# Two fused transformer blocks: attention scores in pairs, a mask inside the row product, and another order at the turn from attention to the mLSTM projections

## The chip, the core and the metric

The kernel runs on one core of a Trainium2 chip. A time is the device time of one execution in microseconds. The engines are TensorE (PE in the profile, its weight loads PEld), VectorE (DVE), ScalarE (ACT), GpSimd (POOL) and SyncE (SP), which issues most weight loads. Each engine runs its own instruction list in order; they wait for each other by semaphores.

## The reference

One token sequence (512 rows of width 1024, 16 meta tokens ahead of them in the first block) goes through two layers. The first (gated linear attention beside sliding-window attention, then a feed-forward part) is not touched. The second is a feed-forward part, a mixer and a feed-forward part. Its mixer, cut to what matters here:

```
proj = u @ w_in                                  # q, k, v, xm, o_pre, ga, gb
# differential attention: 8 heads, two softmaxes each, blocks of 128 queries
s = einsum('bqhcd,bkhcd->bchqk', rope(q), rope(k)) * scale
a = softmax(s)[:, 0] - lam * softmax(s)[:, 1];  ya = a @ v
# mLSTM branch, 4 heads of 256
xc = silu(causal_conv(xm, conv_w, conv_b))       # 4 taps
q, k, v = xc @ w_mq, xc @ w_mk, xm @ w_mv        # per head 256 x 256
dmat = where(tril, b[t] - b[s] + i[s], -inf)     # decay weights from the gates
h = (exp(dmat - m) * (q k^T)) v, divided by a row sum, then normalised
y = (h + ml_skip * xc) * sigmoid(o_pre)
merged = sigmoid(ga) * (ya @ w_proj_a) + sigmoid(gb) * (y @ w_proj_b)
```

## The kernel before, in words

All products of weights are done at fp32 accuracy in three rounded passes (`three`, `project`, L1136 to L1138, and L1142 and L1143 where a split is still being made): a weight chunk of 128 x 1024 and the activation each split into a high part (rounded to fp32r) and a low rest. ACT writes the high part of a weight chunk (`hi`, L564) and DVE the low part (`lo`, L1920), three chunks ahead of PE; `split_hi` (L573, ACT) and `split_lo` (L1926, DVE) do the same for the activation, into `xhi` and `xlo`. A set of splits can overwrite the last only when the chunk that last reads it is done. Products of two activations (scores, weights times values, transposes) are plain fp32.

**Attention units.** After the projection of q, k and v come 32 units (4 query blocks of 128 by 8 heads). Unit i on PE: wait until bank 6 is copied out, project side chunk i (one of ga, gb, xm, o_pre) into bank 6, with the transposes of unit i-1's attention weights (`turn`, L1690) put into its middle; then the scores of unit i+1 (`scores`, L1682: two fp32 products on 64 rows each, the two halves of the array), in each fourth unit the transposes of a group's outputs (L1709), and the product with the values of unit i-1 (`av`, L1699). DVE per unit: two maxima and masks (L2458), a weight split, then the normalised difference of the two softmaxes (L2465 to L2471), and steps of the convolution. ACT per unit: the two exps (L980), a weight split, the copy of unit i-1's transposes (`mixed_out`, L970), and the copy of bank 6 (`store_side`, L949), which POOL then stores to memory. In the first units POOL also turns four keys for the rotary position (`rotate_key`), which `scores` of heads 4 to 7 wait for.

In the last unit ACT, after L970, takes the Silu of the eight convolution results (L991), and only then copies bank 6 and, behind the last projection, unit 31's transposes. PE's list there: `turn(31)`, `av(31)`, and then the QKV chunks (two heads each, four products of 2 x 3 matmuls into banks 0 to 3, L1136 again), which wait for the splits of the convolution result (set 5, L573 and L1926). Those use `xhi`, which projection 31 reads. The copies of QKV's banks (L1015) go to `Ct`, which lies where attention's values `C` were.

**mLSTM weights.** For each of 4 heads, `head_scores` makes for each key block J (512, 384, 256 and 128 query columns) the exponents of the decay weights in bank 0 or 1, from a row product (L1815: `rows4`, 36 rows, picks the head's row of `R4`, which holds its high part in rows 0 to 3 and the rest in 32 to 35) and a product of the identity with the mask `after` (L1816: -2^100 for a key after the query, in the first 128 columns), then the key-query product (L1820). ACT takes the exp (L1063), DVE multiplies the two (L2546), and PE sums over values (L1837). Between the heads' scores PE runs chunks of `w_proj_a`. `R4` lies in `hidhi` and `hidlo`, two tiles each that the feed-forward part uses for its hidden splits; DVE clears it (L2498) and fills it (L2526, L2530).

The scores' place in the unit and the mask's second product, in code:

```python
for i in range(UNITS + 1):
    if i < UNITS:
        ...
        project(C_SIDE + i, bank[6][:, :], between=...).then_inc(chunk_done, 1)
        if i + 1 < UNITS:
            scores(i + 1)
    ...
mm(bank[i % 2][:, 0:N], rows4[:, h, :], R4[J], start=True, stop=False)
mm(bank[i % 2][:, 0:P], ident_r[:, :], after_r[:, :], start=False, stop=True)
```

Of the kernel before, what the change touches and what calls it, by code (L numbers as in the profile page):

```python
# [105 lines left out]
def shape_constants():  # L106
# [15 lines left out]
    out["c_after"] = np.where(i[:, None] > i[None, :], np.float32(-2.0 ** 100), np.float32(0)).astype(np.float32)  # L122
    rows = np.zeros((32 + MH, MH, P), np.float32)
    for h in range(MH):
        rows[h, h] = rows[32 + h, h] = -1
    out["c_rows"] = rows
# [19 lines left out]
def build(nc, t, out):  # L146
    ctx = ExitStack()
    with ctx:
# [34 lines left out]
        rows4 = sb("rows4", [32 + MH, MH, P], F32R)  # L183
# [61 lines left out]
        def source(c):  # L245
# [20 lines left out]
            if C_PB <= c < C_OUT2:  # L266
# [6 lines left out]
                 for n in ("ga", "gb", "op", "xm", "pa")}  # L273

# [142 lines left out]
        after_r = sb("after_r", [P, P], F32R)  # L417
        ident_r = sb("ident_r", [P, P], F32R)
# [10 lines left out]
        R4 = [x[0:32 + MH, m, at:at + T - J * P] for J, (x, m, at) in enumerate(((hidhi, 0, 0), (hidhi, 1, 0), (hidlo, 0, 0), (hidlo, 0, 256)))]  # L429
# [118 lines left out]
        def _(act):  # L548
# [19 lines left out]
            def split_hi(n, kt, src, shift=0.0):  # L568

                if n > 0 and kt == 0:  # L570
                    act.wait_ge(chunk_done, split_last[n - 1] + 1)
                if isinstance(shift, float):
                    ins = A_(xhi[:, kt, :], src, ACT.Copy)  # L573
                else:
                    ins = A_(xhi[:, kt, :], src, ACT.Identity, bias=shift)
                ins.then_inc(s("x_rounded"), 1)
# [394 lines left out]

            UNITS = NB * AH
            for i in range(UNITS + 1):
# [10 lines left out]
                if ph == 0 and 0 <= g < 7:  # L984
                    group_squares(g)
                if i:
                    mixed_out(i - 1)
                if i == UNITS - 1:
                    for kt in range(KT):
                        act.wait_ge(s("conv"), kt + 1)  # L990
                        A_(E[:, kt, :], E[:, kt, :], ACT.Silu).then_inc(s("xc_ready"), 1)  # L991
                if i < UNITS:
                    act.wait_ge(chunk_done, C_SIDE + i + 1)
                    store_side(i, bank[6][:, :])
                if ph == 0 and 0 <= g < 7:
                    group_out(g)


            for kt in range(KT):
                act.wait_ge(s("xc_ready"), kt + 1)  # L1000
                split_hi(5, kt, E[:, kt, :])
            for m in range(3):
# [4 lines left out]
                for pair in range(2):  # L1007
                    c = C_QKV + 2 * m + pair
                    hi(c + AHEAD)
                    for q in range(4):  # L1010
                        if q < 3:
                            act.wait_ge(s("qkv_done"), 3 * (c - C_QKV) + q + 1)
                        else:
                            act.wait_ge(chunk_done, c + 1)
                        A_((Ct, B, Dt)[m][:, 4 * pair + q, :], bank[q][:, :], ACT.Copy).then_inc(s("qkv_out"), 1)  # L1015
# [115 lines left out]
        def _(pe):  # L1131
# [583 lines left out]
            scores(0)  # L1715
# [1067 lines left out]
```

## Time and profile before

| | |
|---|---|
| median of 3 runs | 2007.22 us (2006.17 to 2008.24) |
| profiled execution | 2006.44 us, its span 2004.7 us |
| PE busy | 1957.1 us, 98% |
| DVE, ACT, POOL busy | 57%, 38%, 20% |
| TensorE clock, mean of the span | 0.994 of full |
| DMA | 233.12 MB, 116 GB/s |
| attention units | about 1141 to 1378 us of the span |
| QKV and gates | about 1385 to 1430 us |
| mLSTM weights with w_proj_a | about 1430 to 1545 us |

A row of the timeline gives the start (us from the span's start), the length, the engine, the line, the operation, what it writes and reads, the shape and how many like it are merged; in brackets how long the engine stood idle before it and what ended that. Matmuls overlap in the pipeline, so the interval between two starts says what one costs, not its length; a plain fp32 product shows as two matmul records. "issue" as a releaser means that the profile shows nothing that the engine waited for.

### The profile page before, as it was taken

The numbers are of one execution on the slowest core, as the hardware profiler recorded it, in microseconds if no ns is written. First come the engines' busy times: TensorE is split into PE (matmuls) and PEld (weight loads), VectorE is DVE, ScalarE is ACT, GpSimd is POOL, SyncE is SP. The second block draws the span as 40 slices with busy tenths as digits, with TensorE's granted clock in tenths as the row PEclk, the third lists the DMA queues.
The fourth block names the chain that finished last, engine by engine and source line by source line (L and its number), as shares of the span: only waits on it lengthen the run. The fifth ranks groups of instructions, "written<-read, shape, count | busy, mean of one in ns | idle before, by whom it ended". The sixth has DMA issues, their size and how long they took to land.

```text
span 2004.7 us, 25463 instructions
## 1 busy us (share of the span) xinstructions
PE 1957.1 (98%) x9512; PEld 1569.1 (78%) x9512; DVE 1140.6 (57%) x1734; ACT 766.5 (38%) x1307; POOL 396.0 (20%) x331
## 2 busy tenths in 40 slices
PE   8999999999999999999999999999999999999998
PEld 6876678888887788888888977777677788888887
DVE  7566577667667655453564266564634755444444
ACT  7437342223225222222332344546656342222223
POOL 3000039999200695000000141101000000000000
PEclk9999999999999999999999999999999999999999
DMA  6320246666322564323245433324126423233331
GB/s 171 86 71 22 63 140 206 202 201 206 122 86 73 178 199 139 101 88 105 84 122 137 116 116 116 106 95 137 55 79 202 117 74 105 84 105 93 96 101 56
DMA packets 274991, 233.12 MB, mean 116 GB/s; under 512 B 16632, under 2 KB 248443, under 8 KB 274369
## 3 DMA queue, kind: packets, MB, share of 16 engines
q1 hardware_dynamic: 255792, 166.29, 28.3%
q0 software_dynamic: 17680, 61.41, 9.4%
q10 hardware_dynamic: 1440, 4.40, 1.0%
q8 instruction: 48, 0.79, 0.2%
q14 instruction: 31, 0.25, 0.0%
HBM read 214.95 MB, written 12.58 MB: 114 GB/s over the span
## 4 chain that ended last, share of the span: by engine, by line
PE 90%; DVE 5%; ACT 2%; issue 1%; DMA 1%; ACTq 0%; SPq 0%; DVEq 0%; POOLq 0%
PE bank L1136 25%; PE bank L1138 25%; PE bank L1137 25%; PE bank L1142 2%; PE bank L1143 2%; PE bank L1682 1%; PE bank L1699 1%; PE bank L1584 1%; DVE wlo L1920 1%; PE bank L1837 1%; PE bank L1353 1%; PE bank L1820 1%; PE bank L1192 1%; PE bank L1505 1%; PE bank L1401 1%
## 5 line engine op out<-in xcount | busy, mean ns | idle before, releaser
L1136 PE MATMUL bank<-xhi,whi 128*128 128x512 f32 x1680 | 665.8, 396 | 2.7 <-DVE H L2311 1.6
L1138 PE MATMUL bank<-xhi,wlo 128*128 128x512 f32 x1680 | 655.5, 390 | 0.0
L1137 PE MATMUL bank<-xlo,whi 128*128 128x512 f32 x1680 | 654.4, 390 | 0.0
L1920 DVE TENSOR_TENSOR wlo<-stage,whi 128x1024 fp32r<-128x1024 f32 x309 | 404.6, 1320 | 197.1 <-ACT whi L564 196.8
L564 ACT ACTIVATE whi<-stage 128x1024 fp32r<-128x1024 f32 x309 | 321.3, 1051 | 403.9 <-PE bank L1138 364.9
L1136 PEld LDWEIGHTS bank<-xhi,whi 128*128 128x128 f32 x1680 | 315.9, 188 | 72.2 <-issue 6.5
L1138 PEld LDWEIGHTS bank<-xhi,wlo 128*128 128x128 f32 x1680 | 315.5, 188 | 68.0
L1137 PEld LDWEIGHTS bank<-xlo,whi 128*128 128x128 f32 x1680 | 315.9, 188 | 63.2
L2311 DVE SCALAR_TENSOR_TENSOR H<-bank,sc,H 128x512 f32<-128x512 f32 x304 | 217.8, 746 | 78.4 <-PE bank L1138 76.6
L1136 PE MATMUL bank<-hidhi,whi 128*128 128x512 f32 x532 | 209.4, 394 | 0.0
L1138 PE MATMUL bank<-hidhi,wlo 128*128 128x512 f32 x532 | 208.3, 392 | 0.0
L1137 PE MATMUL bank<-hidlo,whi 128*128 128x512 f32 x532 | 206.9, 389 | 0.0
L2333 DVE TENSOR_TENSOR arena<-bank,arena 128x512 f32<-128x512 f32 x44 | 30.4, 691 | 310.0 <-PE bank L1138 308.3
L2686 POOL TENSOR_TENSOR arena<-arena 128x1024 f32<-128x1024 f32 x63 | 167.9, 2665 | 5.3
L2671 POOL DMA_DIRECT2D arena<-in_w_ada x72 | 42.8, 595 | 429.3 <-DVE xlo L1926 257.7
L1138 PEld LDWEIGHTS bank<-hidhi,wlo 128*128 128x128 f32 x532 | 99.9, 188 | 23.2
L1137 PEld LDWEIGHTS bank<-hidlo,whi 128*128 128x128 f32 x532 | 99.9, 188 | 22.3
L1136 PEld LDWEIGHTS bank<-hidhi,whi 128*128 128x128 f32 x532 | 100.0, 188 | 20.4
L2684 POOL TENSOR_SCALAR arena<-arena,sc 128x1024 f32<-128x1024 f32 x72 | 105.3, 1462 | 5.6 <-DMA arena<-in_w_ada 2.5
L860 ACT ACTIVATE hidhi<-arena 128x512 fp32r<-128x512 f32 x44 | 27.9, 633 | 195.7 <-DVE arena L2333 195.7
L855 ACT ACTIVATE arena<-bank 128x512 f32<-128x512 f32 x44 | 26.3, 598 | 151.0 <-PE bank L1138 150.9
L2696 POOL DMA_DIRECT2D arena<-arena x4 | 2.0, 516 | 362.8 <-ACT arena L928 362.8
(450 smaller groups left out, 2078.1 us busy)
## 6 DMA issues: line engine op xcount, KB each, us to landing
arena<-in_w_ada POOLq DMA_DIRECT2D x72, 512.0 KB, 3.8
stage<-in_w_in SPq DMA_DIRECT2D x71, 512.0 KB, 3.7
stage<-in_w_ff SPq DMA_DIRECT2D x64, 512.0 KB, 4.6
stage<-in_w_gate SPq DMA_DIRECT2D x44, 512.0 KB, 4.3
stage<-in_w_up SPq DMA_DIRECT2D x44, 512.0 KB, 3.7
stage<-in_w_down SPq DMA_DIRECT2D x44, 512.0 KB, 3.8
stage<-in_w_proj_a SPq DMA_DIRECT2D x8, 512.0 KB, 4.1
stage<-in_w_proj_b SPq DMA_DIRECT2D x8, 512.0 KB, 5.0
```

The lines of the kernel that those rows point to most:

```text
L564: A_(whi[:, static % SPLITS, :], stage[:, static % STAGES, :], ACT.Copy).then_inc(chunk_hi, 1)
L1136: mm(out, sh, mh, start=start, stop=False, **kw)
L1137: mm(out, sh, ml, start=False, stop=False, **kw)
L1138: return mm(out, sl, mh, start=False, stop=stop, **kw)
L1142: mm(out, sh, mh, start=start, stop=False)
L1143: mm(out, sl, mh, start=False, stop=False)
L1920: V.tensor_tensor(wlo[:, static % SPLITS, :], stage[:, static % STAGES, :], whi[:, static % SPLITS, :].bitcast(F32), ALU.subtract).then_in ...
L2311: V.scalar_tensor_tensor(out=H[:, x, :], in0=bank[(4 + x) % 8][:, :], scalar=gate(x), in1=H[:, x, :], op0=ALU.mult, op1=ALU.add).then_inc( ...
L2333: V.tensor_tensor(hid_t[j], bank[2 * j + 1][:, :], act_t[j], ALU.mult).then_inc(hid_f32, 1)
L2671: pool.dma_start(st_ada[n % 3], t["w_ada_2"][0, kt * P:(kt + 1) * P, m * D:(m + 1) * D]).then_inc(ring[n % 3], 16)
L2684: link(G.tensor_scalar(dst, st_ada[n % 3], silu_c[:, kt:kt + 1], 0.0, ALU.mult, ALU.add))
L2686: G.tensor_tensor(acc, acc, t_ada, ALU.add).then_inc(s("ada_sum"), 1)
```

## The change

It has five edits.

1. The mask joins the row product. `rows4` and `R4` grow to 128 rows; rows 64 to 127 of `R4` hold `after` (64 rows of two queries' masks) in the first 128 columns and 0 elsewhere, and `rows4` holds weights 1 and 2^76 for them. The second matmul (L1816), `after_r` and `ident_r` go. DVE fills the rows by four copies of 128 columns and three clearing products in place of one cast and four clearing products. The load of the constant rows (POOL's queue) grows from 72 KB to 256 KB.
2. Scores go in pairs: those of units 0 and 1 ahead of projection 0, those of i+1 and i+2 behind projection i for odd i.
3. The eight Silus of the convolution run on ACT in units 20 and 30, four each: the first ahead of the copy of bank 6, three behind it.
4. The first two splits of set 5 go to `hidhi` and `hidlo` in place of `xhi` and `xlo`, and are made in unit 31 (ACT behind the copy of unit 30's transposes, DVE behind unit 31's weights); splits 2 and 3 stand on ACT ahead of the copy of unit 31's transposes.
5. `av(31)` moves behind the second product of the first QKV chunk. ACT waits for it before it copies that product's bank.

```diff
...
     out["c_chunked"] = chunked
-    out["c_after"] = np.where(i[:, None] > i[None, :], np.float32(-2.0 ** 100), np.float32(0)).astype(np.float32)
-    rows = np.zeros((32 + MH, MH, P), np.float32)
+    pair = np.arange(P // 2)[:, None]
+    after = np.zeros((P, P), np.float32)
+    after[P // 2:] = np.where(i[None, :] < 2 * pair, np.float32(-2.0 ** 50),
+                              np.where(i[None, :] == 2 * pair, np.float32(-2.0 ** -26), np.float32(0)))
+    out["c_after"] = after
+    rows = np.zeros((P, MH, P), np.float32)
     for h in range(MH):
         rows[h, h] = rows[32 + h, h] = -1
+        for r in range(P // 2):
+            rows[P // 2 + r, h, 2 * r] = 1
+            rows[P // 2 + r, h, 2 * r + 1] = 2.0 ** 76
     out["c_rows"] = rows
...
         ones = sb("ones", [P, P])
-        rows4 = sb("rows4", [32 + MH, MH, P], F32R)
+        rows4 = sb("rows4", [P, MH, P], F32R)
         par = sb("par", [P, 196])
...
                  for n in ("ga", "gb", "op", "xm", "pa")}
+
+        BESIDE = (5,)
+
+        def split_high(n, kt):
+            return (hidhi if n in BESIDE and kt < 2 else xhi)[:, kt, :]
+
+        def split_low(n, kt):
+            return (hidlo if n in BESIDE and kt < 2 else xlo)[:, kt, :]
...
         after = sb("after", [P, P])
-        after_r = sb("after_r", [P, P], F32R)
-        ident_r = sb("ident_r", [P, P], F32R)
...
         Dv = [arena[:, b * DVW:(b + 1) * DVW] for b in range(NB - 1)] + [arena[:, d0 + 2560:d0 + 2560 + DVW]]
-        R4 = [x[0:32 + MH, m, at:at + T - J * P] for J, (x, m, at) in enumerate(((hidhi, 0, 0), (hidhi, 1, 0), (hidlo, 0, 0), (hidlo, 0, 256)))]
+        R4 = [x[:, m, at:at + T - J * P] for J, (x, m, at) in enumerate(((hidhi, 0, 0), (hidhi, 1, 0), (hidlo, 0, 0), (hidlo, 0, 256)))]
         Wb = [tl(40), tl(41)]
...
-                if n > 0 and kt == 0:
+                if n > 0 and kt == (2 if n in BESIDE else 0):
                     act.wait_ge(chunk_done, split_last[n - 1] + 1)
+                if n == 5:
+                    act.wait_ge(s("xc_ready"), kt + 1)
                 if isinstance(shift, float):
-                    ins = A_(xhi[:, kt, :], src, ACT.Copy)
+                    ins = A_(split_high(n, kt), src, ACT.Copy)
                 else:
-                    ins = A_(xhi[:, kt, :], src, ACT.Identity, bias=shift)
+                    ins = A_(split_high(n, kt), src, ACT.Identity, bias=shift)
                 ins.then_inc(s("x_rounded"), 1)
...
+            def conv_silu(kt):
+                act.wait_ge(s("conv"), kt + 1)
+                A_(E[:, kt, :], E[:, kt, :], ACT.Silu).then_inc(s("xc_ready"), 1)
+
             UNITS = NB * AH
+            SILU_AT = {20: range(4), 30: range(4, KT)}
             for i in range(UNITS + 1):
...
                     group_squares(g)
+                if i == UNITS:
+                    for kt in range(2, 4):
+                        split_hi(5, kt, E[:, kt, :])
                 if i:
                     mixed_out(i - 1)
+                for kt in SILU_AT.get(i, ())[0:1]:
+                    conv_silu(kt)
                 if i == UNITS - 1:
-                    for kt in range(KT):
-                        act.wait_ge(s("conv"), kt + 1)
-                        A_(E[:, kt, :], E[:, kt, :], ACT.Silu).then_inc(s("xc_ready"), 1)
+                    for kt in range(2):
+                        split_hi(5, kt, E[:, kt, :])
                 if i < UNITS:
...
                     store_side(i, bank[6][:, :])
+                for kt in SILU_AT.get(i, ())[1:]:
+                    conv_silu(kt)
                 if ph == 0 and 0 <= g < 7:
...
-            for kt in range(KT):
-                act.wait_ge(s("xc_ready"), kt + 1)
+            for kt in range(4, KT):
                 split_hi(5, kt, E[:, kt, :])
...
                             act.wait_ge(chunk_done, c + 1)
+                        if c == C_QKV and q == 1:
+                            act.wait_ge(s("av_done"), UNITS)
                         A_((Ct, B, Dt)[m][:, 4 * pair + q, :], bank[q][:, :], ACT.Copy).then_inc(s("qkv_out"), 1)
...
             scores(0)
+            scores(1)
             for i in range(UNITS + 1):
...
                     project(C_SIDE + i, bank[6][:, :], between=(lambda kt: turn(i - 1) if kt == KT // 2 else None) if i else None).then_inc(chunk_done, 1)
-                    if i + 1 < UNITS:
+                    if i % 2 and i + 1 < UNITS:
                         scores(i + 1)
+                        scores(i + 2)
                 else:
...
                     group_turn(g)
-                if 1 <= i <= UNITS:
+                if 1 <= i < UNITS:
                     av(i - 1)
...
                         col = (2 * (q // 2) + kt) * MHD + e * P
+                        n = 5 if m < 2 else 6
                         ins = three(bank[q][:, :], whi[:, c % SPLITS, col:col + P], wlo[:, c % SPLITS, col:col + P],
-                                    xhi[:, 2 * head + kt, :], xlo[:, 2 * head + kt, :], kt == 0, kt == 1)
+                                    split_high(n, 2 * head + kt), split_low(n, 2 * head + kt), kt == 0, kt == 1)
                     ins.then_inc(chunk_done if q == 3 else s("qkv_done"), 1)
+                    if k == 0 and q == 1:
+                        av(UNITS - 1)
                 if k == 1:
...
                         pe.wait_ge(s("R_ready"), J + 1)
-                    mm(bank[i % 2][:, 0:N], rows4[:, h, :], R4[J], start=True, stop=False)
-                    mm(bank[i % 2][:, 0:P], ident_r[:, :], after_r[:, :], start=False, stop=True).then_inc(s("wexp_in"), 1)
+                    mm(bank[i % 2][:, 0:N], rows4[:, h, :], R4[J], start=True, stop=True).then_inc(s("wexp_in"), 1)
                     if i >= 2:
...
                 if shift is None:
-                    ins = V.tensor_tensor(xlo[:, kt, :], src, xhi[:, kt, :].bitcast(F32), ALU.subtract)
+                    ins = V.tensor_tensor(split_low(n, kt), src, split_high(n, kt).bitcast(F32), ALU.subtract)
                 else:
...
             dve.wait_ge(s("const_loaded"), 16 * 14)
-            V.tensor_copy(rows4[:, :, :], tl(41)[0:32 + MH, :].rearrange("k (h p) -> k h p", h=MH))
-            V.tensor_copy(ident_r[:, :], ident[:, :])
+            V.tensor_copy(rows4[:, :, :], tl(41).rearrange("k (h p) -> k h p", h=MH))
             junk = tl(26)[:, 0:64]
...
                                            op0=ALU.mult, op1=ALU.add).then_inc(s("am_ready"), 1)
+                if i == UNITS - 1:
+                    for kt in range(2):
+                        split_lo(5, kt, E[:, kt, :])
                 g, ph = divmod(i - 5, 4)
...
-            for kt in range(KT):
+            for kt in range(2, KT):
                 split_lo(5, kt, E[:, kt, :])
...
-            V.tensor_copy(after_r[:, :], after[:, :])
             for J, x in enumerate(R4):
-                V.tensor_scalar(x.rearrange("k (b p) -> k b p", p=P), ident[0:32 + MH, :].unsqueeze(1).to_broadcast([32 + MH, NB - J, P]),
-                                0.0, None, ALU.mult)
+                V.tensor_copy(x[:, 0:P], after[:, :])
+                if J < NB - 1:
+                    V.tensor_scalar(x[:, P:].rearrange("k (b p) -> k b p", p=P), ident[:, :].unsqueeze(1).to_broadcast([P, NB - 1 - J, P]),
+                                    0.0, None, ALU.mult)
             dve.wait_ge(s("act_once"), ONCE["f_softplus"])
...
                 row += rows
-            pool.dma_start(tl(41)[0:32 + MH, :].rearrange("k (h p) -> k h p", h=MH), t["c_rows"]).then_inc(s("const_loaded"), 16)
+            pool.dma_start(tl(41).rearrange("k (h p) -> k h p", h=MH), t["c_rows"]).then_inc(s("const_loaded"), 16)
             pool.dma_start(wgu[:, :], t["w_gate_up"][0]).then_inc(s("const_loaded"), 16)
...
             pool.dma_start(sinks[:, :], t["sinks"].to_broadcast([P, SH])).then_inc(s("const_loaded"), 16)
...
```

## Rows read from the trace of the kernel before

**Rows 1.** The page's chain that ended last, shares of the span by engine.
```profile
PE 90%; DVE 5%; ACT 2%; issue 1%; DMA 1%; ACTq 0%; SPq 0%; DVEq 0%; POOLq 0%
```
**Rows 2.** Window: length, busy PE, PEld, DVE, ACT, POOL, granted clock, DMA share, GB/s.
```profile
1378.50:1385.00 6.50, 3.37 (x22) 3.10 (x21) 1.36 (x4) 6.50 (x14) 0.54 (x1) 0.84 0.33 116
```
**Rows 3.** Timeline of PE from the last projection of the units into QKV.
```profile
1378.32 0.39 PE L1138 MATMUL bank<-xhi,wlo 128*128 128x512 f32 x1
1378.55 1.05 PE L1699 MATMUL bank<-arena 128*128 128x128 f32 x8
1379.44 0.60 PE L1690 MATMUL bank<-ident,arena 128*128 128x128 f32 x4
1383.17 2.08 PE L1699 MATMUL bank<-arena 128*128 128x128 f32 x8 [3.13 <-ACT arena L970]
...
1386.32 0.41 PE L1136 MATMUL bank<-xhi,whi 128*128 128x512 f32 x1
```
**Rows 4.** Timelines of ACT and DVE in unit 31.
```profile
1373.22 0.72 ACT L980 ACTIVATE arena<-arena,small 128x512 f32<-128x512 f32 x1 [2.00 <-DVE small L2461]
...
1376.59 1.28 ACT L991 ACT_TABLE_LOAD   x1
1377.89 4.27 ACT L991 ACTIVATE arena<-arena 128x512 f32<-128x512 f32 x8
...
1375.72 1.22 DVE L1920 TENSOR_TENSOR wlo<-stage,whi 128x1024 fp32r<-128x1024 f32 x1 [2.54 <-ACT whi L564]
...
1377.77 0.75 DVE L2471 SCALAR_TENSOR_TENSOR arena<-arena,small 128x512 f32<-128x512 f32 x1
```
**Rows 5.** Timelines of PE and PEld in the later scores, heads 0 and 1.
```profile
1452.52 4.60 PE L1837 MATMUL bank<-arena 128*128 128x257 f32 x20 [1.12 <-DVE arena L2546]
1457.05 0.50 PE L1815 MATMUL bank<-hidhi,rows 36*128 36x512 f32 x1
...
1457.48 0.19 PEld L1816 LDWEIGHTS bank<-after_r,ident_r 128*128 128x128 f32 x1 [0.25 <-issue]
...
1457.48 0.33 PE L1816 MATMUL bank<-after_r,ident_r 128*128 128x128 f32 x1
1457.64 1.93 PE L1820 MATMUL bank<-arena 128*128 128x512 f32 x4
1459.51 0.44 PE L1815 MATMUL bank<-hidhi,rows 36*128 36x384 f32 x1
```
**Rows 6.** Timeline of PE between projections, units 0, 1, 3 and 30.
```profile
1147.82 0.39 PE L1138 MATMUL bank<-xhi,wlo 128*128 128x512 f32 x1
...
1148.89 0.50 PE L1136 MATMUL bank<-xhi,whi 128*128 128x512 f32 x1 [0.27 <-ACT arena L949]
...
1154.71 0.49 PE L1682 MATMUL bank<-arena 64*128 64x128 f32 x4
1155.13 0.49 PE L1699 MATMUL bank<-arena 128*128 128x128 f32 x2
...
1166.76 0.33 PE L1690 MATMUL bank<-ident,arena 128*128 128x128 f32 x1 [1.70 <-DVE arena L2471]
...
1370.20 0.39 PE L1138 MATMUL bank<-xhi,wlo 128*128 128x512 f32 x1
1370.52 1.13 PE L1682 MATMUL bank<-arena 64*128 64x512 f32 x4
1371.57 1.16 PE L1699 MATMUL bank<-arena 128*128 128x128 f32 x8
1372.49 0.47 PE L1136 MATMUL bank<-xhi,whi 128*128 128x512 f32 x1
```
**Rows 7.** Timeline of DVE at the start: the copy of the constant rows.
```profile
26.63 0.42 DVE L2023 CAST rows<-arena 36x512 fp32r<-36x512 f32 x1 [0.53 <-DMA arena<-in_lambda_k]
```
**Rows 8.** Timeline of PE in the first layer: window scores of two heads.
```profile
179.69 0.73 PE L1401 MATMUL bank<-gg,arena 64*128 64x272 f32 x4
181.12 1.14 PE L1401 MATMUL bank<-gg,arena 64*128 64x272 f32 x4 [0.70 <-DVE small L2165]
```

## The prediction

> **What bounds the kernel now.** I read the page's chain of waits first: PE holds nine tenths of the chain that ended last [rows 1]. So a part of the change is worth what it takes out of PE's own sequence or out of a PE wait; work moved on another engine is worth something only there. Then I cut the stage around the change into windows and looked for stretches in which PE is not full. The 6.5 us in which the attention units end and the QKV products begin stand out: PE is busy for 3.37 us of them, at a mean granted clock of 0.84 [rows 2]. Then the timeline of PE there: the products of unit 30 (L1699), the transposes of unit 31 (L1690), a wait of 3.13 us for ACT, the products of unit 31, then QKV [rows 3]. The timeline of ACT and DVE over the same time shows who is late: ACT loads a table and runs eight Silus before it copies unit 31's transposes (L970) [rows 4]. Last I read PE's timeline of one head of the later scores and of single units [rows 5, 6].
>
> **Part 1: the turn from the units to QKV.** Before, from the start of unit 30's products to the fourth QKV matmul 1386.32 - 1378.55 = 7.77 us pass [rows 3]. Unit 31's products in it stretch to 2.08 us where unit 30's take 1.05: after the wait PE runs near half rate, which with the mean clock of 0.84 [rows 2] says that 1.2 GHz was granted there instead of 2.4, and the row at 1386.32 is back at its usual length.
> After, the Silus lie in units 20 and 30, QKV's first two splits have other buffers and are made during projection 31, and the products of unit 31 come behind the second QKV product. What PE waits for next is DVE's last weights of unit 31 (L2471), for the transposes. That wait I work out on the clock of before. At unit 30 ACT does one Silu before its copy of bank 6 and three behind it: 4.27/8 = 0.53 us each, 1.6 in all, then a table load of 1.28 back to Exp [rows 4]. The row at 1373.22 shows that ACT had waited 2.00 us for DVE before these exps, so it was free at 1371.2. The exps start at 1371.2 + 1.6 + 1.3 = 1374.1, 0.9 later. (Unit 31's scores are there a unit earlier, so DVE is not what delays them.) From DVE's split at 1375.72 to the end of the last weights at 1378.52 it is 2.8 us, and all of that moves by 0.9, to 1379.4. PE meanwhile is 1.2 us early, as unit 30 has no scores behind it any more (part 3): its products of unit 30 start at 1377.4, the transposes could start 0.89 later, at 1378.3, and wait until 1379.5. They take about 0.4, DVE's first low split beside them about 0.6 (half of the 1.22 that the row at 1375.72 has for twice the columns): first QKV matmul at 1380.1, fourth at 1380.8, which is 3.4 after 1377.4. The products of unit 31 still cost 0.9 to 1.0, now at the full clock. Gain: 7.77 - 3.4 - 1.0 = **3.4 us**. With no wait at all it is 4.8; if the wait doubles to 2.4 and the clock falls again (0.7), 1.5. I take 3.4, since each piece has a row.
> The other edits of this part cost nothing. The two splits on ACT and DVE stand behind unit 31's weights on DVE, so they delay nothing that the transposes need; ACT's splits 2 to 7 come 0.53 us apart, and PE's next need, the second head, is two QKV products and unit 31's products later. ACT's new wait for all attention products before it copies the second QKV bank holds only ACT's copies behind it: PE needs that bank again four products on. Unit 20's batch delays unit 21's exps as unit 30's does, but there the transposes come only half a projection later, so 0.9 us is in time. The spill of unit 31's output on POOL comes earlier with ACT's copy, and its big load of the convolution input, which waits for the last products, starts within a microsecond of where it does now.
>
> **Part 2: mask rows.** Each of 16 row products (L1815, 36 rows) loses its second matmul (L1816) and becomes one of 128 rows. In head 1, for 512 columns, L1815 starts 0.43 before L1816 and L1816 0.16 before the key products L1820; the next L1815 follows 1.87 after these [rows 5]. PE's weight load for L1816 stood idle 0.25 us until "issue" [rows 5]: it was not fetched ahead, between a 36-row and a 128-row product. That gap goes too: 512 columns before a change of kind take 0.32 (1370.20 to 1370.52 [rows 6]), so 0.59 becomes 0.32: 0.27 saved. How much the entry from L1820 saves as well no row shows: between nothing and the 0.16 or so by which 1.87 is over twice the 0.85 that part 3 finds for 512 columns. I take 0.33. Heads 1 to 3 run PE without a wait in this stretch, so 12 x 0.33 = **4.0 us**; the lower bound is L1816's own interval, 12 x 0.16 = 1.9, the upper 12 x 0.43 = 5.2. Head 0 gives nothing: PE waits 1.12 us there for DVE's weights (L2546) [rows 5], which stand behind two weight splits on DVE.
> The Trainium skill, TensorEngine Tiling (Array Packing), Key Properties, says that changing the tiling mode drains the engine. By it the upper bound, 5.2, would be the term; the 0.25 us of idle weight load agrees with a drain, but not with how long one is at each of the two edges.
>
> **Part 3: scores in pairs.** Behind an odd unit's projection PE now issues two units' scores, behind an even one none. A unit's scores take 0.42 us at 128 columns and 1.05 at 512, that is 0.21 and 0.21 for every 128 columns [rows 6]; the second of a pair should cost only the latter, and one entry (0.32 against the 0.23 from 1378.32 to 1378.55 [rows 3]) and one exit go. What the second waits for (DVE's reductions of the unit just projected, and in units 5 and 7 POOL's turned keys) is asked for one unit earlier than now; DVE does a unit's reductions as it begins the unit, and POOL turns the keys in the first three units, so I put no wait there. But an even unit is now short: bank 6 must be copied before the next projection, and that takes 1148.89 - 1147.82 = 1.07 us whatever PE does [rows 6]. Before, the gap in the last block was 1372.49 - 1370.20 = 2.29 [rows 6]; now it is 0.23 + 0.89 = 1.12 [rows 3], and the odd gap grows by 0.85: 0.32 gained, three times. With 0.21 less per block for scores and for products, the gap before is 1.86, 1.42 and 1.08, after it is 1.07 each, and the odd one grows by 0.64, 0.43 and 0.12 to 0.21: +0.15 four times, -0.08 four times, -0.3 once where the blocks change, -0.12 twice. The scores put ahead of the first projection cost 0.21, but PE waits 1.70 us in unit 3 for DVE anyway [rows 6], and DVE starts unit 1 up to half a microsecond earlier: +0.3. Together +1.0 + 0.6 - 0.3 - 0.3 - 0.2 + 0.3 = 1.1; less 0.04 for each of 15 second scores, **+0.5 us**. Bounds: 0.1 more for each second score, -1.5 in round numbers with some waiting at the short gaps, and +1.2.
>
> **Part 4: the rest, at 0.** The constant rows grow from 72 to 256 KB. DVE waited 0.53 us for the loads of this queue [rows 7]; if that doubles, DVE is 0.5 late at its mask-row copy, of which 0.2 comes back as one cast is gone, and it next waits for ACT's softplus. Filling the row buffers (four short copies more, one product and one cast less) stands ahead of a DVE wait for ACT's softplus too (L2501). Bounds 0 to -0.7.
>
> **Sum.** 3.4 + 4.0 + 0.5 = 7.9 us. The profiled execution took 2006.44 us (span 2004.7), 0.78 below the median 2007.22; 1998.5 of its own time, so **1999.3 us** for the median. All lower bounds together give a gain of 1.2 (2006.0), all upper ones 11.2 (1996.0).
>
> **Rivals.** (a) Overlap lost. The two matmuls of a score use different halves of the rows and run beside each other. Two such score matmuls of 272 columns take 0.73 us in one place and 1.14 in another [rows 8]: there the second ran behind the first, 0.41 more, nearly the whole length. If queueing four makes all scores run singly, each of 32 units loses 0.21 x blocks: 8 x 0.21 x (1+2+3+4) = 17 us, and the time is 2007.2 - 7.9 + 17 = 2016. It turns slower than before where over half the overlap goes. Against it: behind a full queue, as here, the pairs overlap (1.05 for 512 columns); the 1.14 follows a wait. 4 in 100.
> (b) Table loads that drain. Two more switches to Silu and two back stand among the units now. If each emptied ACT for as long again as it loads, 1.3 us, the copies of bank 6 in units 20 and 30 would be some 1.2 late each, as the first Silu there about fits ahead of the copy, and unit 31's exps 2.6 later, which brings a wait as long as before and the slow clock: part 1 gives about 0, and 7.9 - 3.4 - 2.4 = 2.1 is left: 2005.1. Against it: the load at 1376.59 ends at 1377.87 and the first Silu starts at 1377.89 [rows 4].
> This is a rule of the Trainium skill, ScalarE: Activation LUTs, What ACT_TABLE_LOAD costs: 1283 ns of load and some 1380 ns of drain. The trace has the first and not the second. 6 in 100.
> (c) Small ends: pairs at -1.5, rows at 1.9, the turn at 2.5: a gain of 2.9, 2004.3. For it speaks that the short gaps leave PE at the mercy of ACT's copy; against it the idle weight load. 10 in 100.
>
> **How the numbers follow.** The forecast and what lies around it down to a gain of 4 us gets 80 in 100. About 0.2%, 4 us, is what a measurement of this kernel can tell from no change: faster below 2003.2. (b) and (c) are within it, (a) is slower: 0.80, 0.16, 0.04. The range 1996.0 to 2004.3 runs from all upper bounds to (c).
>
> **What would show it.** Right: PE's idle before unit 31's products is gone, with 1 to 1.5 us left before its transposes; QKV's first matmuls at the full clock; L1820 some 0.32 after a 512-column L1815; gaps of 1.07 us behind even units up to 24. Wrong: no wait before the transposes (gain near 9), or one near 3 us; pairs of scores over 2 us at 512 columns; ACT late with the copy of bank 6 in units 20 or 30.

## The result, and the profile after

| | before | after |
|---|---|---|
| median of runs | 2007.22 us (5 runs, 2004.93 to 2008.24) | **1996.22 us** (5 runs, 1994.45 to 2002.14) |
| ratio of the runs | 1 | 0.995, 95% interval 0.9935 to 0.9965 |
| profiled execution: time, span | 2006.44, 2004.7 us | 2002.14, 2000.4 us |

That is 11.0 us faster (7 to 13 by the interval); 7.9 were forecast. The profiled execution of after is the slowest of its five, and the two spans differ by only 4.3 us. So the comparison goes stage by stage, from starts of matmuls in PE's timeline. "Units" is first score to first product of unit 30, "turn" from there to the fourth QKV matmul, "to heads" from there to the first row product, "heads" from there to the start of the last group of key products.

| us | first score at | units | turn | to heads | heads | mean clock |
|---|---|---|---|---|---|---|
| before | 1142.05 | 236.50 | 7.77 | 57.55 | 67.60 | 0.994 |
| after | 1146.80 | 237.11 | 3.58 | 57.18 | 61.73 | 0.991 |

In after unit 31's products (0.82: 1389.56 to 1390.37 in the rows below) have moved from the turn into the next column. From the first score to the last key products after is 9.8 us shorter. The first layer is where it loses 4.75 again, in lines that the change doesn't touch: over all profiles of this study the first score stands between 1141.5 us (mean clock 0.996) and 1149.1 (0.990), in the main later where the granted clock was lower. Behind the heads after takes 0.8 longer (494.0 us to the end, 493.2 before).

**The chain of waits** is still PE's (answers to [rows 1]):
```profile
PE 89%; DVE 5%; ACT 3%; issue 1%; DMA 1%; ACTq 0%; SPq 0%; DVEq 0%
```
**The turn**, PE's timeline after (to [rows 3]):
```profile
1383.68 0.39 PE L1165 MATMUL bank<-xhi,wlo 128*128 128x512 f32 x1
1383.91 1.05 PE L1726 MATMUL bank<-arena 128*128 128x128 f32 x8
1386.03 0.66 PE L1717 MATMUL bank<-ident,arena 128*128 128x128 f32 x4 [1.06 <-DVE arena L2501]
1386.72 0.47 PE L1163 MATMUL bank<-hidhi,whi 128*128 128x512 f32 x1
...
1387.49 0.39 PE L1163 MATMUL bank<-hidhi,whi 128*128 128x512 f32 x1
...
1389.56 1.06 PE L1726 MATMUL bank<-arena 128*128 128x128 f32 x8
1390.37 0.48 PE L1163 MATMUL bank<-xhi,whi 128*128 128x512 f32 x1
```
The wait of 3.13 us for ACT is gone; 1.06 us for DVE's last weights of unit 31 are left. The granted clock stays at its upper level through the turn (to [rows 2]; same columns):
```profile
1383.00:1386.00 3.00, 1.96 (x13) 1.60 (x11) 2.73 (x6) 3.00 (x7) 0.54 (x1) 1.00 0.06 13
1386.00:1390.00 4.00, 3.94 (x20) 3.23 (x21) 4.00 (x7) 3.46 (x7) 0.00 (x0) 1.00 0.51 187
```
ACT's timeline in units 30 and 31 (to [rows 4]) shows why DVE is late:
```profile
1375.06 1.28 ACT L989 ACT_TABLE_LOAD   x1
1376.36 0.63 ACT L989 ACTIVATE arena<-arena 128x512 f32<-128x512 f32 x1
1377.19 0.60 ACT L964 ACTIVATE arena<-bank 128x512 f32<-128x512 f32 x1 [0.20 <-PE bank L1165]
1377.69 1.66 ACT L989 ACTIVATE arena<-arena 128x512 f32<-128x512 f32 x3
1379.37 1.28 ACT L1000 ACT_TABLE_LOAD   x1
1380.66 0.72 ACT L1000 ACTIVATE arena<-arena,small 128x512 f32<-128x512 f32 x1
```
One Silu fits ahead of ACT's copy of bank 6 (L964), with 0.20 us to spare. Three stand behind it, and with the load back to Exp they push unit 31's exps (L1000) out.

**A wait that is new** stands in unit 21, in PE's timeline, at the transposes of a finished group of heads (L1736):
```profile
1303.93 1.56 PE L1709 MATMUL bank<-arena 64*128 64x384 f32 x8
1306.27 0.66 PE L1736 MATMUL bank<-ident,gg 128*128 128x128 f32 x4 [0.79 <-DVE gg L2461]
```
**One head of the later scores**, PE's timeline (to [rows 5]):
```profile
1457.60 0.59 PE L1847 MATMUL bank<-hidhi,rows 128*128 128x512 f32 x1
1458.03 1.88 PE L1851 MATMUL bank<-arena 128*128 128x512 f32 x4
1459.34 0.74 PE L1847 MATMUL bank<-hidhi,rows 128*128 128x384 f32 x1
1459.92 1.45 PE L1851 MATMUL bank<-arena 128*128 128x384 f32 x4
```
Before, the second key products start here (to [rows 5]):
```profile
1460.04 1.51 PE L1820 MATMUL bank<-arena 128*128 128x384 f32 x4
```
From the first key products to the second it is 1.89 us, before 2.40. The gain lies between the key products and the next row product, 1.87 to 1.31; from that row product of 384 columns to its key products it is 0.58, before 0.53. Only at a head's first row product, which follows sums over values, does that part shrink too, 0.59 to 0.43.

**The softplus.** ACT's timeline ahead of the heads, first of before:
```profile
1429.83 0.63 ACT L1026 ACTIVATE lrT<-tabs 4x512 f32<-4x512 f32 x1
1430.48 1.28 ACT L1027 ACT_TABLE_LOAD   x1
1431.77 0.63 ACT L1027 ACTIVATE lrT<-lrT 4x512 f32<-4x512 f32 x1
1432.42 1.28 ACT L1028 ACT_TABLE_LOAD   x1
```
and of after:
```profile
1431.92 0.63 ACT L1053 ACTIVATE lrT<-tabs 4x512 f32<-4x512 f32 x1
1432.58 0.63 ACT L1054 ACTIVATE lrT<-lrT 4x512 f32<-4x512 f32 x1
1433.23 1.28 ACT L1055 ACT_TABLE_LOAD   x1
```
Before, ACT came out of the Silus and had to load Exp's table here. After, unit 31's exps came last, so the table is there and the first of two loads is gone. PE feels it at transposes that wait for ACT's copies behind the softplus (L1039), before:
```profile
1435.58 2.27 PE L1772 MATMUL bank<-ident,arena 128*128 128x128 f32 x16 [0.84 <-ACT arena L1039]
```
and after, without a wait:
```profile
1436.68 1.99 PE L1804 MATMUL bank<-ident,arena 128*128 128x128 f32 x16
```

### The profile page after: what moved, and what is told of

Same layout as the page of the kernel before. It is cut to its first block, busy times and chain, and to the rows that moved or that the text cites. A ratio compares the mean times of both kernels' runs of the same rounds, so it can differ in the third digit from the quotient of the medians.

```text
span 2000.4 us, 25435 instructions
## 1 busy us (share of the span) xinstructions
PE 1950.1 (97%) x9496; PEld 1573.6 (79%) x9496; DVE 1139.2 (57%) x1735; ACT 769.1 (38%) x1309; POOL 395.4 (20%) x331
## 4 chain that ended last, share of the span: by engine, by line
PE 89%; DVE 5%; ACT 3%; issue 1%; DMA 1%; ACTq 0%; SPq 0%; DVEq 0%
PE bank L1163 25%; PE bank L1165 25%; PE bank L1164 25%; PE bank L1169 2%; PE bank L1170 2%; PE bank L1709 1%; PE bank L1611 1%; DVE wlo L1951 1%; PE bank L1868 1%; PE bank L1380 1%; PE bank L1726 1%; PE bank L1532 1%; PE bank L1851 1%; PE bank L1219 1%; PE bank L1428 1%
```

## The experiments

Each kernel was profiled once on a chip; the last two were also timed against before in five rounds. The measure is the stage lengths, as total times carry the first layer's spread. "Units" has a spread of its own: in every kernel PE waits for DVE in unit 3, ahead of unit 2's transposes, for 1.26 to 2.10 us, and these start 24.42 to 25.13 us after the first score, in kernels with pairs and without. So up to 0.7 us of a difference in "units" can come from there.

| us | first score | units | turn | to heads | heads | mean clock |
|---|---|---|---|---|---|---|
| mask rows alone (r1) | 1148.95 | 236.45 | 7.77 | 58.72 | 61.77 | 0.989 |
| pairs alone (r2) | 1145.66 | 235.75 | 7.68 | 57.48 | 67.61 | 0.992 |
| after without pairs (r3) | 1143.01 | 237.07 | 2.36 | 57.18 | 61.75 | 0.995 |
| Silus, splits, products alone (r4) | 1141.49 | 237.41 | 2.37 | 57.17 | 67.62 | 0.996 |
| 128 rows, second matmul kept (r5) | 1142.29 | 236.71 | 6.94 | 58.90 | 63.09 | 0.993 |
| 36 rows, no second matmul (r6) | 1143.58 | 238.31 | 7.37 | 58.45 | 65.88 | 0.993 |
| after, late pairs (r7) | 1144.19 | 235.37 | 3.60 | 57.19 | 61.74 | 0.993 |
| after, Silus 5, 2, 1 (r8) | 1149.08 | 236.72 | 2.02 | 57.19 | 61.73 | 0.990 |
| late pairs, small batches (r9) | 1143.15 | 235.24 | 2.03 | 57.18 | 61.74 | 0.992 |
| after once more (r10) | 1145.35 | 236.99 | 3.59 | 57.19 | 61.73 | 0.992 |

**r1, mask rows alone.** The parts of the diff on rows4, R4, c_after, c_rows and head_scores on the kernel before; no other.

> Stages are read from the trace: units (first score to the first product of unit 30), turn (from there to the fourth QKV product), QKV to the first row product, heads (first row product to the last key product). Before: 236.5, 7.8, 57.6, 67.6 us; after: 237.1, 3.6, 57.2 (with unit 31's products, 0.9), 61.7. Theory: the 5.9 us in the heads come wholly from the mask rows, as a 36-row product among 128-row ones costs PE on entry and on exit: heads 61.7, the other three as before, time 5.9 below the kernel before. Rival: the mask rows give the 4.0 of the forecast and the rest came with the other edits, which change what DVE and ACT do in these heads: heads 63.6. And if the longer load of the constant rows costs something, the first score stands later than the 1142.05 of before, by up to the 4.75 that the kernel after showed.

Heads 61.77: the theory. All but 0.04 of the 5.87 comes with the mask rows. The 58.72 to the heads was not expected. It is the turn's slow clock: after the wait of 3.13 us, windows of r1 show the lower level up to about 1396:
```profile
1389.00:1392.00 3.00, 1.98 (x9) 1.98 (x10) 1.48 (x3) 3.00 (x8) 0.54 (x1) 0.50 0.23 87
1392.00:1396.00 4.00, 4.00 (x12) 3.08 (x12) 4.00 (x7) 3.55 (x7) 0.92 (x1) 0.53 0.34 67
1396.00:1400.00 4.00, 4.00 (x19) 3.31 (x18) 0.56 (x1) 1.80 (x4) 0.00 (x0) 1.00 1.00 376
```
Before, QKV's fourth matmul was back at full speed [rows 3], here only the tenth, at 1395.73.

**r2, pairs alone.** On before:
```
             scores(0)
+            scores(1)
...
-                    if i + 1 < UNITS:
+                    if i % 2 and i + 1 < UNITS:
                         scores(i + 1)
+                        scores(i + 2)
```


> Theory: the pairs by themselves cost 0.6 us where the forecast had them save 0.5, as each second score costs its full 0.21 per block and the gap behind an even unit stays at 1.07: units 237.1, and the turn still ends when ACT's Silus do, so units and turn together 244 to 245 (before 244.3). Rival: the pairs save what was forecast and the 0.6 belongs to the Silus of units 20 and 30: units 235.8 to 236. The other stages as before.

The rival: units 235.75, 0.75 saved, of which 0.10 stands ahead of unit 2's transposes and 0.65 behind; 0.5 was forecast. From transposes to transposes units 27 and 28 take 8.95 + 6.91 = 15.86 us instead of 8.12 + 8.10, units 19 and 20 15.00 instead of 15.11, units 11 and 12 14.15 instead of 14.07: +0.36, +0.11, -0.08, where 0.32, 0.15 and -0.08 were forecast.

**r3, after without pairs** (r2's edit taken back).

> Everything but the pairs. Theory: units 236.5 (before's, within 0.3, plus whatever unit 20's Silus cost), the turn shorter than after's 3.6 by the 1.2 us of scores that PE does behind unit 30 in place of waiting, 2.5; units and turn together 239.0 to 239.5 against 240.7 after: the pairs then cost the kernel after 1.2 to 1.7. Rival: unit 31's scores coming a unit later delay its weights as much, the wait before its transposes stays 1 us, and the turn is 3.6: units and turn 240.1. QKV to heads 57.2, heads 61.7 by both.

The theory: units 237.07 (0.7 of it unit 20's Silus, see r4), turn 2.36, together 239.43. The kernel after takes 1.26 us more. Of these, 0.56 stands ahead of unit 2's transposes (25.13 us after the first score, 24.57 here), in the wait that varies with and without pairs; 0.7 is what the pairs cost it. No wait is left before unit 31's transposes, as PE does unit 31's scores behind projection 30 while DVE finishes the weights. With pairs it has done them already, and waits.

**r4, Silus, split buffers and later products alone** (the kernel without pairs, mask rows taken back too).

> The Silus, the split buffers and the later products alone. Theory: turn as in the kernel without pairs (2.5 to 3.6), and QKV to the first row product 57.2, which with 0.9 of unit 31's products in it is 1.2 less than before: the Silus' table is no longer switched between QKV and the softplus. Heads as before, 67.6. Rival: that 1.2 came from the mask rows' buffers, filled with one DVE instruction less ahead of the softplus: then 58.4 here, and 56.3 in the kernel with the mask rows alone.

57.17: the theory; the 1.2 us ahead of the heads come with these edits. That it is the Silus' place, and not the splits' or the products', rests on the load that is gone and the wait that went with it. PE's transposes of unit 20 to those of unit 21 take 8.68 us here, 8.67 in r3 and 7.96 before: the batch in unit 20 costs 0.7 by itself, 0.86 with pairs (9.46 in after, 8.60 in r2).

**r5 and r6, the two halves of the mask rows.** r5, on before (cut; the constant rows, their load and copy and the clearing of R4 go from 36 to 128 rows with it):
```
-        rows4 = sb("rows4", [32 + MH, MH, P], F32R)
+        rows4 = sb("rows4", [P, MH, P], F32R)
...
-        R4 = [x[0:32 + MH, m, at:at + T - J * P] for ...
+        R4 = [x[:, m, at:at + T - J * P] for ...
```
r6, on before:
```
-                    mm(bank[i % 2][:, 0:N], rows4[:, h, :], R4[J], start=True, stop=False)
-                    mm(bank[i % 2][:, 0:P], ident_r[:, :], after_r[:, :], start=False, stop=True).then_inc(s("wexp_in"), 1)
+                    mm(bank[i % 2][:, 0:N], rows4[:, h, :], R4[J], start=True, stop=True).then_inc(s("wexp_in"), 1)
```


> The kernel before, with the row product padded with zeros from 36 to 128 rows and the mask's own matmul kept. Theory (the 36-row product costs PE on its way in and out, the second matmul next to nothing): the time from one head's key product to the next falls from 2.40 to about 2.0 at the second and from 1.91 to about 1.5 at the third, as against 1.89 and 1.41 in the kernel after; heads 62.5 to 63.5 where before has 67.6 and after 61.7. Rival (the second matmul is what cost): heads 67.0 to 67.6.

> The kernel before without the second matmul, 36 rows kept; the mask on later positions is left out. Theory: only the second matmul's own interval goes, 0.16 in each of 12: heads 65.5 to 66 (before 67.6). Rival (the second matmul carried the cost, by the idle weight load at its entry): heads 61.7 to 62.5. Both r5 and r6 in the middle, 64 to 65, would say that each edge between a 36-row and a 128-row product costs, and that the two edits share it.

The theory in both. PE's timeline of r5:
```profile
1458.23 1.93 PE L1820 MATMUL bank<-arena 128*128 128x512 f32 x4
1459.60 0.74 PE L1815 MATMUL bank<-hidhi,rows 128*128 128x384 f32 x1
1460.18 0.22 PE L1816 MATMUL bank<-after_r,ident_r 128*128 128x128 f32 x1
1460.23 1.51 PE L1820 MATMUL bank<-arena 128*128 128x384 f32 x4
```
and of r6:
```profile
1460.88 0.49 PE L1815 MATMUL bank<-hidhi,rows 36*128 36x512 f32 x1
1461.31 1.98 PE L1819 MATMUL bank<-arena 128*128 128x512 f32 x4
1463.22 0.44 PE L1815 MATMUL bank<-hidhi,rows 36*128 36x384 f32 x1
1463.59 1.56 PE L1819 MATMUL bank<-arena 128*128 128x384 f32 x4
```
Key products to key products: 2.00 in r5, 2.28 in r6, against 2.40 before and 1.89 after. With 128 rows 0.40 go and with the second matmul 0.12, together about the 0.51 of after. Where they go stands in the timeline of weight loads (PEld). Before:
```profile
1458.13 0.19 PEld L1820 LDWEIGHTS bank<-arena 128*128 128x128 f32 x1 [0.24 <-issue]
...
1459.50 0.18 PEld L1815 LDWEIGHTS bank<-hidhi,rows 36*128 36x128 f32 x1 [0.76 <-issue]
```
r6:
```profile
1463.22 0.18 PEld L1815 LDWEIGHTS bank<-hidhi,rows 36*128 36x128 f32 x1 [0.76 <-issue]
```
after:
```profile
1459.31 0.19 PEld L1847 LDWEIGHTS bank<-hidhi,rows 128*128 128x128 f32 x1 [0.24 <-issue]
```
A load of 36 rows behind products of 128 leaves PEld idle for 0.76 us; one of 128 rows starts after the 0.24 that stand between the key products' own loads too (1458.13).

The 238.31 of r6's units is not the edit's doing. Its wait in unit 3 is 1.92 us, as in r4; but behind it PE's granted clock fell, and unit 2's transposes to unit 3's took 8.21 in place of 6.6 us:
```profile
1169.00:1172.00 3.00, 3.00 (x10) 2.33 (x9) 1.11 (x2) 1.99 (x6) 1.96 (x2) 0.57 0.02 5
```
In r4 the clock stayed at its upper level there.

**r7, late pairs.** On after:
```
+            PAIR_FROM = 17
...
             scores(0)
-            scores(1)
...
-                    if i % 2 and i + 1 < UNITS:
+                    if i < PAIR_FROM and i + 1 < UNITS:
+                        scores(i + 1)
+                    elif i % 2 and i + 1 < UNITS:
                         scores(i + 1)
                         scores(i + 2)
```


> The kernel after, with single scores up to unit 17 and pairs behind units 17 to 29. Theory (pairs lose where an even unit's gap without scores is already short, gain in the last block, and what they gain ahead of unit 31 comes back as a wait for its weights): unit 15 to 16 as without pairs, the transposes of unit 16 at 122.0 after the first score (123.6 in the kernel after, 0.3 of it the wait in unit 3), those of unit 30 at 232.5, the wait before unit 31's transposes still 1.0; units and turn 239.2 to 239.5 (after 240.7). Rival (the saving moves into a longer wait): 240 to 240.7, wait above 1.5.

The theory: transposes of unit 16 at 121.86, of unit 30 at 232.17, units and turn 238.97, a little under the range. Of the 1.72 less than in after, 0.71 is unit 3's wait and 1.0 the later pairs. The wait is as long as before, as ACT's and DVE's work on unit 31 moves with PE.

**r8, Silus 5, 2, 1.** On after:
```
-            SILU_AT = {20: range(4), 30: range(4, KT)}
+            SILU_AT = {22: range(5), 27: range(5, 7), 30: range(7, KT)}
```


> The kernel after, with five Silus in unit 22, two in 27 and one in 30. Theory (four Silus and a table load ahead of unit 21's exps made the group's transposes wait 0.79; three Silus too many in unit 30 make unit 31's wait): no wait for DVE in units 20 to 31, unit 20 to 21 takes 8.60 as with pairs alone (9.46 in after), the wait of 1.06 before unit 31's transposes falls under 0.2: units and turn 238.7 to 239.0, against 240.7. Rival (any batch costs its two table loads, wherever it stands): the 0.8 turns up again behind units 22 or 27.

Half and half. Both waits are gone (unit 20 to 21 in 8.61, units and turn 238.74), but PE waits for DVE again three units behind the batch of five, in unit 25:
```profile
1337.56 1.02 PE L1709 MATMUL bank<-arena 64*128 64x512 f32 x4
1339.51 0.66 PE L1736 MATMUL bank<-ident,gg 128*128 128x128 f32 x4 [0.92 <-DVE gg L2461]
```
The sum came out as forecast only because unit 3's wait was 0.5 shorter than in after. DVE's timeline shows why a delay is kept (its reductions of the scores of two units that follow each other):
```profile
1323.86 0.68 DVE L2488 CUSTOM_DVE_ANT_0 arena<-bank,arena 128x512 f32<-128x512 f32 x1
...
1331.99 0.69 DVE L2488 CUSTOM_DVE_ANT_0 arena<-bank,arena 128x512 f32<-128x512 f32 x1
```
From one to the next 8.13 us, with no idle time ahead of either: the loop through DVE's reductions, ACT's exps and DVE's weights is as long as PE's unit in the last block (15.9 to 16.2 us for two). So it has next to no slack to make up what a batch delays.

**r9, late pairs and small batches; r10, after again.** r9 is r7 with
```
-            SILU_AT = {20: range(4), 30: range(4, KT)}
+            SILU_AT = {11: range(1), 15: range(1, 3), 19: range(3, 4), 23: range(4, 5), 27: range(5, 7), 30: range(7, KT)}
```


> Pairs of scores from unit 17 on as in the kernel with late pairs, and the Silus in small batches: one in units 11, 19, 23 and 30, two in 15 and 27. Theory (ACT has 1.5 us free ahead of its copy of bank 6 and 3 us behind it, so one or two Silus with their two table loads fit where four or five do not, and DVE's and ACT's chain is not late at the next group's transposes): no wait for DVE from unit 3 to unit 31's transposes; units and turn 236.8 to 237.4, against 240.7 in the kernel after, 239.0 with late pairs alone and 244.3 before; about 3.7 us faster than the kernel after and 13 to 15 faster than before by the medians. Rival (every batch leaves the chain late by its table loads): 0.8 or more at a group's transposes again, units and turn 238 or more.

> The kernel after once more, on the chip of the version with late pairs and small batches. By the theory units and turn 240.5 to 240.8, QKV to the first row product 57.2, heads 61.7 as in its first profile, all three within 0.3; the first score stands wherever the granted clock of the first layer puts it (1141.5 to 1149.1 so far), earlier with a higher mean clock; the median 10 to 11 us under before. If instead the first layer is late because of this kernel's longer load of constant rows, the first score is at 1146 or later again.

r9: units and turn 237.27, the theory; behind unit 3 the profile shows no wait of PE's up to QKV. Median 1994.42 us (1992.97 to 1995.69) against before's 2009.1 on that chip, ratio 0.9923 (0.9909 to 0.9936). r10: 1998.47 us, ratio 0.9941 (0.9928 to 0.9955), its four later stages within 0.12 us of after's first profile, the first score at 1145.35. So r9 beats the kernel after by 4.0 us, and before by 14.7.

PE's timeline of r9's turn:
```profile
1378.39 1.05 PE L1728 MATMUL bank<-arena 128*128 128x128 f32 x8
1379.28 0.60 PE L1719 MATMUL bank<-ident,arena 128*128 128x128 f32 x4
1379.65 0.47 PE L1163 MATMUL bank<-hidhi,whi 128*128 128x512 f32 x1
```
Products, transposes and QKV follow each other without a wait.

## Why the prediction was right, and where it was off

**Direction and time.** 1996.22 lies 0.2 us inside the fast edge of the range and 3.1 us below the forecast. By the stages, with unit 31's products put back to the turn: turn 7.77 - 3.58 - 0.82 = 3.4, heads 5.9, to heads 57.55 - 57.18 + 0.82 = 1.2, units -0.6: 9.8. Of the -0.6, -0.4 stands in unit 3's wait and -0.9 in unit 20's batch; the pairs give 0.65 back. The medians say 11.0 and, in r10, 10.6. That the time is still inside the range is partly luck: part 2 went past its own upper bound and 1.2 us were on no list, while the upper bounds of the turn and of the pairs, which that edge also holds, were not reached.

**Part 1, 3.4 forecast, 3.4 measured.** Each piece stands in the rows: the wait of 1.2 that was worked out is 1.06, the first QKV matmul follows 0.69 behind the transposes' start, the clock stays at its upper level. Two things in it were wrong. "0.9 us is in time" for unit 20's batch looked at that unit's own transposes, which come half a projection later; late were the transposes of the group of heads in unit 21 (L1736), which come right behind the projection, wait for DVE's L2461 and were on nobody's list. That is 0.7 to 0.9 us (r4, r3, after). And the prediction asked who else gains or loses by the Silus' place only among what follows at once. The table they leave in ACT was read by the softplus 50 us later: 1.2 us that no step had, the load of 1.28 in the rows above.

**Part 2, 4.0 forecast, 5.9 measured**, more than the 5.2 given as upper bound. That the row product should match its neighbours was right, and so nearly was that head 0 gives nothing (0.25 of the 5.87 in its stretch from first row product to first row product, 13.18 to 12.93). The step that failed is "how much the entry from L1820 saves as well no row shows". A row did: PEld's 0.76 us of idle before the 36-row weights at 1459.50, which the prediction didn't read, as it looked at PEld for L1816 alone. The entry was sized at 0 to 0.16. In r5 it measures 0.50 (1.87 to 1.37 from key products to row product), and the way on to the next key products gives 0.10 of that back (0.53 to 0.63). The other three heads share 5.62: 0.47 for each of their 12 products, not 0.33. And the 0.27 on the way out, the larger term of the 0.33, is not there: the idle 0.25 before L1816 was read as a gap between kinds, but 0.24 stands between the key products' own loads as well, r6 saves only 0.12 without the second matmul, and from a 512-column row product to its key products after takes 0.43, not 0.32. So the term that was put at next to nothing gave the 0.40, and the one that was counted on at most the 0.12: that the forecast of 4.0 came as near to 5.9 as it did is luck.
The Trainium skill's rule that a change of tiling mode drains TensorE (TensorEngine Tiling (Array Packing), Key Properties) agrees on the way in, if 36 rows among 128 are such a change, which no run here shows by itself: 1.91 from key products to row product in r6, 1.31 in after. On the way out r6 and after both take 0.43 for 512 columns, so no cost of that edge shows. The 0.25 us of idle that the prediction took to agree with the rule says nothing for it, as it stands between equal shapes too. The prediction kept the rule for the upper bound alone.

**Part 3, +0.5 forecast.** Alone the pairs save 0.65 behind unit 2's transposes (r2), by the couples of units worked out. In company they save nothing: from unit 2's transposes to unit 30's after gains 0.5 on r3 (208.8 against 209.3), and then waits 1.2 longer at unit 31's. The prediction had both terms, in two parts: PE "1.2 us early" in part 1, the saved entries in part 3. It never set them against each other, and so missed that without pairs units and turn are 0.7 shorter (1.26 with the difference in unit 3's wait).

**Part 4** cannot be told apart from the first layer's spread. Against a cost of the longer load speaks that DVE's copy of the mask rows starts at 26.77 without a wait, where it had 0.53 before [rows 7]:
```profile
26.77 0.42 DVE L2054 CAST rows<-arena 128x512 fp32r<-128x512 f32 x1
```
The first score came at 1142.3 to 1149.1 in the eight profiles with the longer load and at 1141.5 to 1145.7 in the four without. The lost clock stands well behind that copy and comes with the short load too: from 140 to 160 us the mean granted clock is 0.83 in r1, r2 and r8 and full in before, from 260 to 280 us 0.91 in r1, r2, r8 and after and full in before, and r2 has the short load. The medians (11.0 and 10.6) are no smaller than the sum of the stages behind (9.8), which speaks against a lasting loss ahead of them. What sets the clock there was not tried and stays open.

**Rivals.** (a) Overlap lost: no. A pair of scores at 512 columns takes 1.91 us in after, one alone 1.05 [rows 6]; the second adds 0.86, four times 0.21:
```profile
1367.77 1.99 PE L1709 MATMUL bank<-arena 64*128 64x512 f32 x8
1369.68 0.66 PE L1736 MATMUL bank<-ident,gg 128*128 128x128 f32 x4
```
(b) Tables that drain: no. The load at 1375.06 ends at 1376.34 and the Silu starts at 1376.36; the 1.38 us of drain that the Trainium skill adds (ScalarE: Activation LUTs, What ACT_TABLE_LOAD costs) stand in no row. (c) Small ends: no.

## What to carry to other kernels

Read the weight loads' own timeline wherever a matmul with other row counts stands between others, and set the idle time there beside that between neighbours of one shape: the excess shows what the change of shape costs, and rows of zeros can be cheaper than fewer rows. Before work is moved on an engine with tables, list which table it leaves for each later user, and which chain of engines is as long as the bounding engine's own loop: there a delay is kept until the next wait, units later. When two edits both bring the same engine forward, ask what it will wait for with both: here a saving of 0.65 alone became a loss of 0.7 in company.

## What the hardware showed that was not expected

A row product of 36 rows among products of 128 costs 0.40 us more than the same product padded to 128 with zeros (2.40 against 2.00 from key products to key products), though it has less than a third of the rows. Other row counts were not tried.

The wait of 3.13 us before QKV costs more than itself, and not always the same. Behind it PE ran at the lower of the two clock levels (0.50 of 2.4 GHz in r1's window) for about 3 us before and for about 6 in r1. The time from unit 30's products to the first row product was 65.2 to 66.5 us in the five kernels with that wait. In the other seven, with a wait of 1.06 or none, it varies by 0.03 at most among alike kernels: 60.76, 60.78 and 60.79 in after, r10 and r7, 59.54 twice in r3 and r4, and 59.21 twice in r8 and r9.
